# A delta-rule solve: diagonal blocks of 16 by substitution on VectorE, the last three doubling levels on TensorE

## The chip, the cores and the metric

The kernel runs on one core of a Trainium2 chip. The time is the device time of one launch in microseconds (us), the median of several runs. One execution of the kernel was also recorded by the hardware profiler; its rows are what this document reads. In them PE is TensorE, PEld its weight loads, DVE is VectorE, ACT ScalarE, POOL GpSimd and SP the engine that issues most transfers.

## The reference

One layer of a hybrid decoder on 512 tokens of width 1024: RMSNorm, one input projection, three kinds of heads side by side (softmax attention with forget gates, "fox"; retention; gated delta rule, "GDN"), an output projection, then a routed mixture of 32 experts. The part at issue is in the GDN heads, 4 heads, with the sequence cut into chunks of C = 64:

```
lower = where(strict, (kb @ k^T) * decay, 0)          # per head and chunk, 64 x 64
a_mat = lower + eye(64)
sol   = triangular_solve(a_mat, [v*beta | kb*exp(gc)], lower, unit_diagonal)
u0, w = split(sol)                                    # then a scan over the chunks
```

## The kernel before

**Granules.** The input projection is the first long stretch of TensorE work. It is cut into 30 granules (two for each of 15 groups of up to 260 columns; 8 more follow for the output projection). The product is taken in three terms from a high and a low part of activations and weights. Each granule is 48 matmuls of 256 columns (kind "n": tokens in rows, four tiles b = 0 to 3) or 24 of 512 (kind "t", turned: b = 0 and 1), line 792. Groups 12 (granules 24, 25) and below down to 8 are "n", groups 13 and 14 (26 to 29) "t". For each granule, SP loads the raw weights into a ring of three buffers, ScalarE copies the high part (`whi`, line 1255), GpSimd subtracts to get the low part (`wlo`, line 1555, "wlo(g)" for granule g). `wlo(g + 2)` is issued in GpSimd's turn g; TensorE waits for wlo(g) before granule g, and SP waits for `wlo_done` of granule g - 3 before it loads g.

**Tasks between granules.** `AFTER[g]` lists tasks behind granule g. All engines walk through the same list in the same order, each doing its part of every task, and meet through semaphores and through PSUM banks that are handed out in the order of the lists (`tensor_orders`). "evac" moves a group's result out of PSUM. Those of the solve, in which two token tiles of 128 (a pair, pr = 0 or 1, each tile holding two chunks for each of the four heads) are treated together:

- "dec", "decx" and GpSimd's `masked`: the decay matrices `Dm` and their strict form `Ym`.
- "prep": TensorE forms KK and QK; VectorE writes `Nm` (= lower, transposed), then starts the inverse with blocks of two, adds the identity and transposes (`uinit`), and writes `attnT`. GpSimd waits for `uinit` before its wlo, and afterwards multiplies `qT` by the row decays.
- "lv", level 0 to 5: with Y = N X and X' = X + U (mask Y), the size of the inverted blocks doubles from 2 to 64. 32 small matmul passes for Y, a mask on VectorE, 32 for X', a sum and two transposes on VectorE. One level stands between two granules.
- "fin": the inverse times the right sides (`wT`, `u0`).

Pair 0: "prep" behind granule 17, levels behind 18 to 23. Pair 1: "prep" behind 24, levels behind 25 to 29. On GpSimd, the rotation of the retention queries and keys (`rotary`, lines 1595 to 1600, six operations each) belongs to turns 21 (rq) and 23 (rk). In the turn whose list has "fin" of pair 0, it first does `masked` for tiles 2 and 3; in the turn with "prep" it waits for that task's signal before wlo.

VectorE links dependent operations with `link(...)`: the operation signals a semaphore, and the engine waits for it before the next.

After the projection come fox attention with the GDN scan and retention, the output projection, routing, and the experts in 16 pairs, whose weights (96 MB) are loaded as TensorE frees their buffers.

Of the kernel before, what the change touches and what calls it, by code (L numbers as in the profile page):

```python
# [23 lines left out]
F32 = mybir.dt.float32  # L24
# [27 lines left out]
LEVELS = 6  # L52
HB = P // 2
# [45 lines left out]
for _i in range(LEVELS):  # L99
    AFTER[18 + _i].append(("lv", 0, _i))  # L100
AFTER[23] += [("dec", 2), ("dec", 3), ("decx", 2)]
AFTER[24] += [("fin", 0), ("prep", 2)]
for _i in range(LEVELS - 1):
    AFTER[25 + _i].append(("lv", 1, _i))
AFTER[26].append(("silu",))
AFTER[29] += [("lv", 1, LEVELS - 1), ("fin", 1)]
# [18 lines left out]
def tensor_orders():  # L125

    a, b = [], []
    for g in range(GR_IN):
# [3 lines left out]
        for task in AFTER[g]:  # L132
# [80 lines left out]
def constant_table():  # L213
# [46 lines left out]
def build(nc, consts, x, turned, lead, w_in, foxb, alog, dtb, gnw, w_out, n2w, rgw, rgb, rew, reb,  # L260
# [13 lines left out]
    with ExitStack() as ctx:  # L274
# [17 lines left out]
        nM = const("nM", "p (l n) -> p l n", dict(l=LEVELS - 1))  # L292
# [64 lines left out]
        small = at("small", [P, 1024], R9 + 16 * KB)  # L357
        attnT = at("attnT", [P, T, NH, P], R5)
# [10 lines left out]
        UP, DN = slice(0, HB), slice(HB, P)  # L369
        rqT = at("rqT", [P, 2, S], R4)  # L370
# [19 lines left out]
        def sml(a, n):  # L390
            return small[:, a:a + n]
# [27 lines left out]
        vb_done = sem("vb_done"); s_bw = sem("s_bw"); s_cB = sem("s_cB"); s_gB = [sem(f"s_gB{t}") for t in range(T)]; xe_done = sem("xe_done")  # L419
# [106 lines left out]

        cbd = nc.dram_tensor("cbd", [2, NH * T, P], F32, kind="Internal")
# [49 lines left out]
        def _(sp):  # L577
# [177 lines left out]
        def _(pe):  # L755
# [85 lines left out]
            def task(k):  # L841
# [37 lines left out]
                elif k[0] == "lv":  # L879
                    _, pr, lv = k  # L880
                    for i in range(2):
                        t = 2 * pr + i
                        if lv:
# [11 lines left out]
                    for i in range(2):  # L895
# [4 lines left out]
                        elif lv:  # L900
                            pe.wait_ge(u_turned, 2 * (LEVELS - 2) * pr + 2 * (lv - 1) + i + 1)
# [1409 lines left out]
```

## Time and profile before

| what | value |
|---|---|
| median of 3 runs (lowest, highest) | 591.59 us (591.48, 592.23) |
| span of the profiled execution | 589.4 us |
| between span and median | 2.2 us |
| TensorE busy | 562.9 us, 96% of the span |
| VectorE, ScalarE, GpSimd busy | 259.9, 192.8, 183.1 us |
| moved by DMA | 152.67 MB |

The span runs from the first to the last recorded instruction; a program's time holds a little more. The profile has no time of its own for the execution beyond the span. Times of single instructions are counted from the span's start. A busy share says how long an engine had work, not whether it set the end.

### The profile page before, as it was taken

Reading aid. Unit: us, or ns where it says so; the run is one execution under the profiler, and the core shown is the slowest. Engines: PE = TensorE matmul, PEld = TensorE weight load, DVE = VectorE, ACT = ScalarE, POOL = GpSimd, SP = SyncE. Lnnn points to the kernel's source line nnn. Section 1 sums busy time; section 2 is a strip of 40 time slices with the busy share of each in tenths; the row PEclk is TensorE's granted clock in tenths of the full one; section 3 lists DMA queues with packets and bytes.
Section 4 is the critical chain, followed back from the end, with each engine's and each line's share of the span. In section 5 each row is a group of like instructions: output and inputs, shape, how many; then the busy total and the mean of one; then the engine's idle time right before and its main releaser. Section 6 shows DMA issues by size and latency. Waiting matters only on the chain.

```text
span 589.4 us, 11310 instructions
## 1 busy us (share of the span) xinstructions
PE 562.9 (96%) x4579; PEld 431.1 (73%) x4579; DVE 259.9 (44%) x622; ACT 192.8 (33%) x409; POOL 183.1 (31%) x126
## 2 busy tenths in 40 slices
PE   8999999999999999999999999989999999978894
PEld 7988887999999888666789997556566656644541
DVE  6698543782258333765421174223223323221126
ACT  6655455622124523356444312111111211110113
POOL 3443434273567534333552101111211111210021
PEclk9999999999999999999999999999999999999998
DMA  8866543422220310016989588999999999999986
GB/s 333 350 206 175 165 149 87 140 73 74 72 61 15 97 52 33 2 33 275 402 251 392 215 332 312 410 425 426 425 424 428 422 427 423 425 425 426 415 331 233
DMA packets 32083, 152.67 MB, mean 259 GB/s; under 512 B 8759, under 2 KB 12511, under 8 KB 25376
## 3 DMA queue, kind: packets, MB, share of 16 engines
q1 hardware_dynamic: 27360, 143.77, 63.2%
q0 software_dynamic: 4528, 8.15, 3.7%
q8 instruction: 37, 0.61, 0.4%
q14 instruction: 14, 0.11, 0.1%
q10 hardware_dynamic: 144, 0.03, 0.0%
HBM read 143.78 MB, written 16.27 MB: 272 GB/s over the span
## 4 chain that ended last, share of the span: by engine, by line
PE 76%; DMA 14%; DVE 4%; issue 2%; ACT 1%; POOL 1%; SPq 0%; DVEq 0%; POOLq 0%; ACTq 0%
PE bank L792 33%; PE bank L839 8%; DMA w<-in_expert_w_dram 8%; PE bank L1226 7%; DMA xg<-h2d,tok 6%; PE bank L1185 5%; PE bank L1200 5%; PE bank L817 2%; PE bank L1124 2%; PE bank L1138 2%; PE bank L1118 1%; PE bank L1238 1%; PE bank L1094 1%; PE bank L943 1%; PE bank L1010 1%
## 5 line engine op out<-in xcount | busy, mean ns | idle before, releaser
L1555 POOL TENSOR_TENSOR wlo<-raw,whi 128x1024 fp32r<-128x1024 f32 (+1 forms) x24 | 59.2, 2467 | 79.4 <-ACT whi L1255 75.3
L1682 POOL DMA_INDIRECT yd<-oy,dst x15 | 15.2, 1011 | 163.2 <-DVE oy L2217 152.5
L1200 PE MATMUL bank<-w,xT 128*64 128x256 f32 x512 | 58.1, 380 | 4.0 <-DMA w<-in_expert_w_dram 4.0
L1226 PE MATMUL bank<-w,hidT 128*64 128x512 f32 x256 | 58.5, 598 | 1.4 <-ACT hidT L1532 1.4
L1185 PE MATMUL bank<-w,xT 128*64 128x256 f32 x512 | 58.1, 380 | 1.7 <-issue 1.7
L792 PE MATMUL bank<-wlo,hHi 128*128 128x256 f32 (+2 forms) x192 | 55.9, 291 | 0.0
L1185 PEld LDWEIGHTS bank<-w,xT 128*64 128x64 f32 x512 | 36.9, 137 | 26.0 <-issue 10.1
L1200 PEld LDWEIGHTS bank<-w,xT 128*64 128x64 f32 x512 | 36.5, 137 | 22.9 <-DMA w<-in_expert_w_dram 4.9
L2195 DVE SCALAR_TENSOR_TENSOR hid<-bank,slot,sa 128x256 f32<-128x256 f32 x16 | 10.8, 673 | 93.1 <-issue 90.6
L792 PE MATMUL bank<-whi,hHi 128*128 128x256 f32 (+1 forms) x176 | 50.4, 287 | 0.0
L792 PE MATMUL bank<-whi,hLo 128*128 128x256 f32 (+1 forms) x176 | 49.6, 282 | 0.0
L792 PE MATMUL bank<-hHi,wlo 128*128 128x512 f32 x112 | 44.2, 394 | 0.0
L1527 ACT ACTIVATE sa<-bank,slot 128x256 f32<-128x256 f32 x16 | 7.6, 474 | 104.9 <-PE bank L1185 104.9
L1255 ACT ACTIVATE whi<-raw 128x1024 fp32r<-128x1024 f32 (+1 forms) x25 | 26.5, 1061 | 43.4 <-PE bank L792 40.0
L792 PE MATMUL bank<-hHi,whi 128*128 128x512 f32 x96 | 38.4, 400 | 0.5 <-POOL wlo L1555 0.5
L1226 PEld LDWEIGHTS bank<-w,hidT 128*64 128x64 f32 x256 | 16.9, 136 | 29.8 <-issue 27.4
L792 PE MATMUL bank<-hLo,whi 128*128 128x512 f32 x96 | 37.6, 391 | 0.0
L792 PE MATMUL bank<-whi_tight,hHi 128*128 128x256 f32 (+1 forms) x112 | 36.9, 329 | 0.5 <-issue 0.4
L792 PEld LDWEIGHTS bank<-wlo,hHi 128*128 128x128 f32 x192 | 36.2, 189 | 0.5
L792 PE MATMUL bank<-whi_tight,hLo 128*128 128x256 f32 (+1 forms) x112 | 35.1, 314 | 0.0
L1773 DVE SCALAR_TENSOR_TENSOR cacc<-bank,lead_in,cacc 128x511 f32<-128x511 f32 (+2 forms) x36 | 26.5, 747 | 18.2 <-ACT cacc L1337 17.1
L792 PEld LDWEIGHTS bank<-whi,hHi 128*128 128x128 f32 x176 | 33.2, 189 | 0.4
(385 smaller groups left out, 1146.3 us busy)
## 6 DMA issues: line engine op xcount, KB each, us to landing
w<-in_expert_w_dram SPq DMA_DIRECT2D x43, 2048.0 KB, 20.3
raw<-in_w_in_dram SPq DMA_DIRECT2D x24, 512.0 KB, 4.0
w<-in_expert_w_dram SPq DMA_DIRECT2D x10, 1024.0 KB, 7.8
yd<-zt SPq DMA_DIRECT2D x8, 512.0 KB, 5.1
yt<-yd SPq DMA_DIRECT2D x4, 1024.0 KB, 8.1
raw<-in_w_in_dram SPq DMA_DIRECT2D x6, 520.0 KB, 5.5
xt<-in_turned_dram SPq DMA_DIRECT2D x4, 512.0 KB, 6.8
X<-in_x_dram SPq DMA_DIRECT2D x4, 512.0 KB, 10.4
```

What stands on the lines that cost most here:

```text
L792: m = pe.matmul(o, l, r, start=(at == 0 and c == 0 and i == 0), stop=(at == parts - 1 and kc == chunks[-1] and i == 2), skip_group_check=True)
L817: m = pe.matmul(tiles[b][:, 0:w], l, r, start=(kc == 0 and i == 0), stop=(kc == KC - 1 and i == 2), skip_group_check=True)
L839: return pe.matmul(o, l, r, start=True, stop=True)
L1124: m = pe.matmul(pb[0][:, at + a:at + b], rows[:, t, :, :], TG[:, t, q:q + 1, a:b], start=(t == 0), stop=(t == T - 1), skip_group_check=True)
L1138: m = pe.transpose(pb[1 + c // 4][:, (c % 4) * P:(c % 4 + 1) * P], xg[s][:, c * P:(c + 1) * P], ident)
L1185: m = pe.matmul(pb[3][r, 0:FF], xT[:, c, r], w1[u % 4][:, e, c * FF:(c + 1) * FF], start=(c == 0), stop=(c == KC - 1), skip_group_check=True)
L1200: m = pe.matmul(pb[7][r, 0:FF], xT[:, c, r], w3[u % 4][:, e, c * FF:(c + 1) * FF], start=(c == 0), stop=(c == KC - 1), skip_group_check=True)
L1226: m = pe.matmul(pb[5 + n][r, :], hidT[:, c, r], w2[s][:, n, (2 * e + c) * 512:(2 * e + c + 1) * 512], start=(c == 0), stop=(c == 1), skip_ ...
L1255: e.activation(high_of(g), raw_of(g), ACT.Copy).then_inc(whi_done, 1)
L1555: pool.tensor_tensor(low_of(g), raw_of(g), high_of(g).bitcast(F32), ALU.subtract).then_inc(wlo_done, 1)
L1682: pool.indirect_dma_start(yd.ap()[:, :], bass.IndirectOffsetOnAxis(ap=dst_i[o][:, 0:1].bitcast(U32), axis=0), oy[o][:, :], None, bounds_ch ...
L1773: j = dve.scalar_tensor_tensor(out=a[:, s:S], in0=psum(name)[:, 0:S - s], scalar=PCW[:, 3 - s, blk:blk + 1], in1=a[:, s:S], op0=ALU.mult, ...
```

## The change

The inverse of each 16 x 16 diagonal block is now computed by VectorE, and the doubling starts from blocks of 16, so levels 0, 1 and 2 go for both pairs.

- "prep" masks the diagonal blocks out of `Nm` (`blk16`) and folds them with two reductions into `diag`, 128 partitions x 8 (two tiles, four heads) x 16. SP writes it to DRAM (`nbd`, 64 KB) and reads it back in eight transfers, each broadcasting one group of 16 rows to the 16 partitions that hold it, 8 KB to a partition (`spread`, over the place of `Ym` and `Dm`). So each partition holds all 16 rows of its own block.
- "solve" runs the substitution, step b = 1 to 15: a multiplication of 8 x b elements, whose second operand steps by 512 bytes through `spread`, and a reduction of 8 x (b + 1). Every operation is linked to the one before it. Two masked multiplications and two transposes then give `Uc` and `Xc` for level 3.
- `AMID` allows a task inside a granule, behind one of its tiles. Level 3 of pair 0 stands in the middle of granule 21, level 4 behind it, level 5 behind 22; "fin" and pair 1's "prep" move from behind 24 to behind 23; level 3 of pair 1 stands in the middle of granule 27, level 4 behind it, level 5 behind 28, "fin" behind 29.
- GpSimd's turn with "prep" waits for `rows_done` in place of `uinit`. SP's part (`blocks_round`) stands behind its loads of granules 21 and 27.

```diff
@@ -96,14 +98,25 @@
-for _i in range(LEVELS):
-    AFTER[18 + _i].append(("lv", 0, _i))
-AFTER[23] += [("dec", 2), ("dec", 3), ("decx", 2)]
-AFTER[24] += [("fin", 0), ("prep", 2)]
-for _i in range(LEVELS - 1):
-    AFTER[25 + _i].append(("lv", 1, _i))
+AFTER[18].append(("solve", 0))
+AMID = {g: {} for g in range(GR_IN)}
+AMID[21][1] = [("lv", 0, 3)]
+AFTER[21].append(("lv", 0, 4))
+AFTER[22] += [("lv", 0, 5), ("dec", 2), ("dec", 3), ("decx", 2)]
+AFTER[23] += [("fin", 0), ("prep", 2)]
+AFTER[24].append(("solve", 1))
...
-AFTER[29] += [("lv", 1, LEVELS - 1), ("fin", 1)]
+AMID[27][0] = [("lv", 1, 3)]
+AFTER[27].append(("lv", 1, 4))
+AFTER[28].append(("lv", 1, 5))
+AFTER[29].append(("fin", 1))
+BLOCKS_AT = {21: 0, 27: 1}
+def tasks_of(g):
+    return [k for b in sorted(AMID[g]) for k in AMID[g][b]] + AFTER[g]
...
@@ -228,10 +241,11 @@
-    put("nM1", -((row % 2 == 0) & (blk == row + 1)).astype(np.float32))
+    put("blk16", -(row // SB == blk // SB).astype(np.float32))
+    put("unit16", -(row % SB == np.arange(SB)[None, :]).astype(np.float32))
...
-    for n in range(LEVELS - 1):
+    for n in range(SOLVED, LEVELS - 1):
...
@@ -367,6 +385,8 @@
+        spread = at("spread", [P, SB, 2 * NH, SB], R4 + 12 * KB)
+        eights = lambda a: sml(a, 2 * NH * SB).rearrange("p (c n) -> p c n", c=2 * NH)
...
@@ -401,6 +419,7 @@
+        diag, inv, prods = eights(640), eights(768), eights(896)
...
@@ -524,6 +543,7 @@
+        nbd = nc.dram_tensor("nbd", [2, P, 2 * NH * SB], F32, kind="Internal")
...
@@ -622,15 +642,28 @@
                                  cbd.ap()[0:1].rearrange("o (t h) p -> o h t p", h=NH)[:, h].broadcast_to([P, T, P])
-                                 ).then_inc(s_cB, 16)
+                                 ).then_inc(s_spread, 16)
 
...
 
+            def blocks_round(pr):
+                sp.wait_ge(rows_done, pr + 2)
+                sp.dma_start(nbd.ap()[pr], small[:, 640:768]).then_inc(s_bw, 16)
+                for t in (2 * pr, 2 * pr + 1):
+                    wait_read(sp, ("QK", t))
+                sp.wait_ge(s_bw, 32 + 16 * (pr + 1))
+                for d in range(P // SB):
+                    src = nbd.ap()[pr:pr + 1, d * SB:(d + 1) * SB, :].rearrange("o k n -> o (k n)")
+                    sp.dma_start(spread[d * SB:(d + 1) * SB, :, :, :].rearrange("p k c n -> p (k c n)"),
+                                 src.broadcast_to([SB, SB * 2 * NH * SB])).then_inc(s_spread, 16)
             sp.wait_ge(zero_set, 1)
...
                 granule(g)
+                if g in BLOCKS_AT:
+                    blocks_round(BLOCKS_AT[g])
                 if g == 11:
...
@@ -880,7 +913,7 @@
-                        if lv:
+                        if lv > SOLVED:
...
@@ -897,8 +930,8 @@
-                        elif lv:
-                            pe.wait_ge(u_turned, 2 * (LEVELS - 2) * pr + 2 * (lv - 1) + i + 1)
+                        elif lv > SOLVED:
+                            pe.wait_ge(u_turned, 2 * (LEVELS - 2 - SOLVED) * pr + 2 * (lv - 1 - SOLVED) + i + 1)
...
@@ -922,7 +955,7 @@
-                    granule(g)
+                    granule(g, between=lambda b: [task(k) for k in AMID[g].get(b, ())])
...
@@ -1606,7 +1639,7 @@
                     if ("prep", t) in AFTER[g]:
-                        pool.wait_ge(uinit, t + 2)
+                        pool.wait_ge(rows_done, t // 2 + 2)
                 if ("decx", 0) not in AFTER[g]:
...
@@ -1882,14 +1915,12 @@
-                        dve.tensor_tensor(Yc[i][UP, :, :], Nm[i][UP, :, UP], half(const("nM1"), UP), ALU.mult)
-                        j = dve.tensor_tensor(Yc[i][DN, :, :], Nm[i][DN, :, DN], half(const("nM1"), DN), ALU.mult)
+                        for r in (UP, DN):
+                            j = dve.tensor_tensor(Xc[i][r, :, :], Nm[i][r, :, r], half(const("blk16"), r), ALU.mult)
...
-                        j = dve.tensor_tensor(Uc[i], Yc[i], id64.unsqueeze(1).broadcast_to([P, NH, HB]), ALU.add)
-                    link(j)
-                    for i in range(2):
-                        dve.transpose(Xc[i], Uc[i]).then_inc(uinit, 1)
+                        j = dve.tensor_reduce(diag[:, NH * i:NH * i + NH, :], Xc[i].rearrange("p h (d n) -> p h n d", n=SB), AX_X, ALU.add)
+                    j.then_inc(rows_done, 1)
...
@@ -1898,10 +1929,26 @@
+                elif k[0] == "solve":
+                    pr = k[1]
+                    unit = const("unit16").unsqueeze(1).broadcast_to([P, 2 * NH, SB])
+                    dve.tensor_copy(inv[:, :, 0:1], unit[:, :, 0:1])
+                    link(dve.tensor_copy(prods, unit))
+                    dve.wait_ge(s_spread, 16 * NH + 16 * (P // SB) * (pr + 1))
+                    for b in range(1, SB):
+                        link(dve.tensor_tensor(prods[:, :, 0:b], inv[:, :, 0:b], spread[:, 0:b, :, b].rearrange("p k c -> p c k"), ALU.mult))
+                        link(dve.tensor_reduce(inv[:, :, b], prods[:, :, 0:b + 1], AX_X, ALU.add))
+                    places = const("blk16", "p (d n) -> p d n", dict(n=SB)).unsqueeze(1).broadcast_to([P, NH, HB // SB, SB])
+                    for i in range(2):
+                        rows = inv[:, NH * i:NH * i + NH, :].unsqueeze(2).broadcast_to([P, NH, HB // SB, SB])
+                        j = dve.tensor_tensor(Uc[i].rearrange("p h (d n) -> p h d n", n=SB), rows, places, ALU.mult)
+                    link(j)
+                    for i in range(2):
+                        dve.transpose(Xc[i], Uc[i]).then_inc(uinit, 1)
...
-                        mask = nM[:, lv, :].unsqueeze(1).broadcast_to([P, NH, HB])
+                        mask = nM[:, lv - SOLVED, :].unsqueeze(1).broadcast_to([P, NH, HB])
...
```

The rest of the diff names the new constants, semaphores and views, makes `tasks_of` the list that the bank order and VectorE walk, and makes fox attention wait for the renamed semaphore of the cB loads.

## Rows read from the trace of the kernel before

**Rows 1.** The page: DMA rate in 40 slices, and the chain by engine.
```profile
GB/s 333 350 206 175 165 149 87 140 73 74 72 61 15 97 52 33 2 33 275 402 251 392 215 332 312 410 425 426 425 424 428 422 427 423 425 425 426 415 331 233
...
PE 76%; DMA 14%; DVE 4%; issue 2%; ACT 1%; POOL 1%; SPq 0%; DVEq 0%; POOLq 0%; ACTq 0%
```

**Rows 2.** TensorE's timeline: start, duration (us), instructions merged where alike.
```profile
2.00 5.87 PE L918 MATMUL bank<-zt 128*128 128x256 bf16 x30 [2.00 <-DVE zt L1720]
...
123.38 0.37 PE L792 MATMUL bank<-whi,hHi 128*128 128x256 f32 x1
...
129.25 0.33 PE L839 MATMUL bank<-Xm,Nm 64*64 64x64 f32 x4
...
137.40 1.15 PE L839 MATMUL bank<-Xm,Nm 64*64 64x64 f32 x32
...
139.69 0.38 PE L792 MATMUL bank<-whi,hHi 128*128 128x256 f32 x1
...
186.16 0.36 PE L792 MATMUL bank<-whi_tight,hHi 128*128 128x256 f32 x1
...
194.38 0.50 PE L792 MATMUL bank<-hHi,whi_tight 128*128 128x512 f32 x1
...
200.12 0.45 PE L839 MATMUL bank<-Xm,Nm 64*64 64x64 f32 x8
```

**Rows 3.** VectorE's timeline, behind the masks of "prep", pairs 0 and 1.
```profile
125.42 0.76 DVE L1889 TENSOR_TENSOR Xm<-Ym,CT 128x256 f32<-128x256 f32 x2
...
187.67 0.76 DVE L1889 TENSOR_TENSOR Xm<-Ym,CT 128x256 f32<-128x256 f32 x2
```

**Rows 4.** VectorE's timeline in the routing: linked operations; TG steps by 16 bytes.
```profile
342.83 0.29 DVE L2097 TENSOR_TENSOR rtB<-rtB,rtA 128x128 f32<-128x128 f32 x1
343.16 0.29 DVE L2098 TENSOR_TENSOR rtB<-rtB,CT 128x128 f32<-128x128 f32 x1
...
352.59 0.22 DVE L2146 TENSOR_TENSOR rtA<-rtA 128x64 f32<-128x64 f32 x1
...
353.16 0.28 DVE L2148 TENSOR_TENSOR rtA<-rtA,TG 128x64 f32<-128x64 f32 x1
```

**Rows 5.** The page: DMA issues, KB each, median us to landing.
```profile
cbd<-small SPq DMA_DIRECT2D x2, 8.0 KB, 3.3
```

**Rows 6.** Tile cB: issues (ns min/median/max, first and last start us), landings.
```profile
L623 SPq DMA_DIRECT2D cB<-cbd x4: 438/507/508, 102.2 to 103.8; - x4
...
DMA to landing us min/median/max: 4.7/5.3/6.1
```

**Rows 7.** VectorE's timeline, beside GpSimd's operations of rows 8.
```profile
45.97 2.41 DVE L1801 SCALAR_TENSOR_TENSOR small<-small 128x32 f32<-128x32 f32 x1
...
173.95 7.39 DVE L1869 TENSOR_SCALAR Dm<-mix,small 128x128 f32<-128x128 f32 x8
...
189.16 2.12 DVE L1897 SCALAR_TENSOR_TENSOR attnT<-bank,small,Dm 128x128 f32<-128x128 f32 x8
```

**Rows 8.** GpSimd's timeline.
```profile
45.92 2.41 POOL L1555 TENSOR_TENSOR wlo<-raw,whi 128x1024 fp32r<-128x1024 f32 x1 [2.05 <-ACT whi L1255]
...
139.20 2.38 POOL L1555 TENSOR_TENSOR wlo<-raw,whi 128x1024 fp32r<-128x1024 f32 x1 [4.91 <-ACT whi L1255]
...
174.33 1.11 POOL L1595 TENSOR_TENSOR rtmp<-rk,CT 128x512 f32<-128x512 f32 x1
...
180.00 1.26 POOL L1600 TENSOR_TENSOR rk<-rtmp,rtmp 128x512 f32<-128x512 f32 x1
...
189.31 2.41 POOL L1555 TENSOR_TENSOR wlo<-raw,whi_tight 128x1024 fp32r<-128x1024 f32 x1 [3.84 <-DVE Xm L1892]
191.67 2.51 POOL L1572 TENSOR_TENSOR qT<-qT,mix 128x512 f32<-128x512 f32 x2
...
201.42 2.39 POOL L1555 TENSOR_TENSOR wlo<-raw,whi_tight 128x1024 fp32r<-128x1024 f32 x1 [4.86 <-ACT whi_tight L1255]
```

**Rows 9.** Busy time by window: PE, PEld, DVE, ACT, POOL, PEclk, DMA share, GB/s.
```profile
581.50:586.00 4.50, 0.00 (x0) 0.00 (x0) 4.40 (x9) 2.46 (x6) 0.00 (x0) 0.76 0.43 162
```

More of the change, by code:

```diff
@@ L52 @@
 LEVELS = 6
+SB = 16
+SOLVED = 3
 HB = P // 2
@@ L131, in tensor_orders @@
             (b if g == 2 else a).extend(("y", g // 2, n) for n in range(T if kind == "n" else 2))
-        for task in AFTER[g]:
+        for task in tasks_of(g):
             if task[0] == "rb":
@@ L203 @@
 for _name, _n in [("ident", P), ("eps", 1), ("eps128", 1), ("ones", P), ("iota", 2 * CAP), ("tok1", T), ("thr", 8),
-                  ("desc", NE), ("gdesc", NG), ("rankm", P), ("tri", P), ("strict", P), ("negmask", P), ("nM1", HB), ("id64", HB),
-                  ("cos", T * 32), ("sin", T * 32), ("nM", (LEVELS - 1) * HB), ("dm", NH * S)]:
+                  ("desc", NE), ("gdesc", NG), ("rankm", P), ("tri", P), ("strict", P), ("negmask", P), ("blk16", HB), ("unit16", SB), ("id64", HB),
+                  ("cos", T * 32), ("sin", T * 32), ("nM", (LEVELS - 1 - SOLVED) * HB), ("dm", NH * S)]:
     CONST[_name] = (_at, _n)
@@ L291, in build @@
         ones, eps = const("ones"), const("eps")
-        nM = const("nM", "p (l n) -> p l n", dict(l=LEVELS - 1))
+        nM = const("nM", "p (l n) -> p l n", dict(l=LEVELS - 1 - SOLVED))
         id64 = const("id64")
@@ L357, in build, with sml @@
         small = at("small", [P, 1024], R9 + 16 * KB)
+        def sml(a, n):
+            return small[:, a:a + n]
         attnT = at("attnT", [P, T, NH, P], R5)
@@ L388, in build @@
         ssn, rn, ssx4 = keep[:, 88:104], keep[:, 104:120], keep[:, 120:136]
-        def sml(a, n):
-            return small[:, a:a + n]
         GAB = sml(0, 32).rearrange("p (t n) -> p t n", t=T)
@@ L418, in build @@
         cum_done = sem("cum_done"); rows_done = sem("rows_done"); cexp_done = sem("cexp_done")
-        vb_done = sem("vb_done"); s_bw = sem("s_bw"); s_cB = sem("s_cB"); s_gB = [sem(f"s_gB{t}") for t in range(T)]; xe_done = sem("xe_done")
+        vb_done = sem("vb_done"); s_bw = sem("s_bw"); s_spread = sem("s_spread"); s_gB = [sem(f"s_gB{t}") for t in range(T)]; xe_done = sem("xe_done")
         um_low = sem("um_low"); u_turned = sem("u_turned"); sq_done = sem("sq_done"); root_done = sem("root_done"); ss_read = sem("ss_read"); kt_done = sem("kt_done")
@@ L1931, in _ @@
             for g in range(GR_IN):
-                for k in AFTER[g]:
+                for k in tasks_of(g):
                     task(k)
@@ L1957, in _ @@
                         if u == 0:
-                            dve.wait_ge(s_cB, 16 * NH)
+                            dve.wait_ge(s_spread, 16 * NH + 32 * (P // SB))
                             dve.wait_ge(rot_done, 2)
```

## Prediction

> **What bounds the kernel now.** I read the forty slices and the chain of waits first [rows 1]. The chain lies on TensorE for 76% of the span. From about slice 25 the DMA engines move some 425 GB/s, so the expert stage is bound by weight transfers, but these are released by semaphores that TensorE's progress sets. Time won or lost between 120 and 235 us should therefore reach the end one for one. I read that stretch in the timelines of TensorE, VectorE and GpSimd [rows 2, 3, 7, 8]. TensorE does not idle there: a granule of the normal kind takes 5.87 us (123.38 to 129.25), one of the turned kind 5.74 (194.38 to 200.12), and between granules stands one doubling level, 137.40 to 139.69, so 2.29 us [rows 2]. VectorE and GpSimd have gaps of some us between tasks, and those gaps are what the change draws on.
>
> **What goes.** Levels 0, 1 and 2 of two pairs: 6 x 2.29 = 13.7 us of TensorE [rows 2]. Their VectorE work (masks, sums, transposes) hid in VectorE's gaps and gives nothing. The nM1 mask, the identity sum and the two transposes in "prep" are replaced by a blk16 mask of the same shape and two reductions, at the price of the two operations of 128x256, 0.76 us [rows 3]. The kept levels 3 to 5 cost what they did; putting level 3 inside a granule costs a break that the present ones have too.
>
> **The new chain behind "prep".** rows_done comes 0.76 us after the last mask: 125.42 + 0.76 = 126.2 for pair 0; for pair 1, 187.67 + 0.76 is 2.3 us after the granule behind "prep" started (186.16) [rows 2, 3]. I call that start T0. SP then writes 64 KB to DRAM: 3.3 us by the write of the cumulative rows [rows 5]. It reads back eight pieces, 1 MB in all. The cB loads move the same 1 MB, also broadcast from such a scratch, in four; the last is issued 1.6 us after the first and lands at most 6.1 us later [rows 6]: 7.7 us. The bounds are 4.7 (all eight overlap like the quickest quarter) and 10.1 (eight issues of 0.5 us, the last landing after 6.1). I take 7.7: the spread stands at 137.2 for pair 0, at T0 + 13.3 for pair 1. The raw loads queued behind these on SP have several us in hand, and so has wlo of the next granule, which now waits on rows_done instead of the transposes, so earlier.
>
> **The substitution.** Thirty operations, each waiting for the one before it. A linked operation of 128 elements recurs every 0.33 us at 0.29 of busy time, so a link adds 0.04; 64 elements are 0.22 busy [rows 4]. That gives 0.19 + 0.0011 per element. The multiplications have 8b elements, the reductions 8(b+1), for b = 1 to 15: 960 + 1080 = 2040. So 30 x 0.19 + 2040 x 0.0011 = 7.9 us. An operand with a step of 16 bytes costs 0.28 instead of 0.22 for 64 elements [rows 4]; the spread's step is 512 bytes, no row shows that one, and the same surcharge on 960 elements is 0.9. The bounds are 7.9 and, if the longer step is twice as dear, 9.7; I take 8.8, by the nearest row. Behind the loop come two 128x256 multiplications, 0.76, and the first transpose, for which I take half of that: 1.2 us until level 3 may begin [rows 3].
>
> **The shared port.** This is what decides. While GpSimd runs an operation of two SBUF operands, a VectorE operation that reads two SBUF tensors waits for its end: L1801, 32 elements wide, took 2.41 us from 45.97, beside the wlo operation from 45.92 to 48.33 [rows 7, 8]. Between back-to-back GpSimd operations VectorE gets one operation in: eight that need 0.27 us each took 7.39 beside the rotary [rows 7]. A PSUM operand is free of it: attnT, eight in 2.12 us, ran beside wlo from 189.31 [rows 7, 8]. The levels that go read PSUM; the multiplications inv x spread read SBUF twice. Each wlo that falls into the loop costs it 2.2 us.
>
> **Pair 0.** TensorE now reaches level 3 at 123.38 + 3.5 x 5.87 = 143.9. The wlo of granule 21 begins 1.8 us after granule 19 (139.20 against 137.40), so at 135.1 + 1.8 = 136.9, and ends at 139.3; that of granule 22 begins 1.3 after granule 20 (201.42 against 200.12), at 142.3 [rows 2, 8]. The loop starts at 139.3, takes 8.8 and loses 2.2: 150.3; with the tail 151.5. Stall 7.6 us. With the spread at its early bound (134.2) it does 2.7 us of steps before the first lock and ends at 148.6: 4.7. With the late one (139.9) 8.2.
>
> **Pair 1.** "prep" moves from behind granule 24 to behind 23, so rotary(rk), wlo(25) and qT change their order on GpSimd. There it is: wlo(25), which waits for rows_done, T0 + 2.3 to 4.7; rotary 6.9 (174.33 to 181.26) to 11.6; qT 2.5 to 14.1; wlo(26) 2.4 to 16.5, and 16.7 with the slots that VectorE takes; wlo(27) straight behind, to 19.2 [rows 8]. TensorE wants wlo(26) at T0 + 2 x 5.87 = 11.7 and waits 5.0 us. In the kernel before, rotary(rk) was over long before "prep". VectorE gets two multiplications in between these operations (0.8 us of its 8.8) and is free from 19.3; wlo(28) locks it once more, since granule 26 ends at 22.5: 19.3 + 8.0 + 2.2 + 1.2 = T0 + 30.7. Without any wait TensorE would be at level 3 of pair 1 at 11.7 + 5.74 + 2.87 = 20.3. So pair 1 costs 10.4 us, 5.0 of it before granule 26 and 5.4 at level 3. Early bound 9.3 (more slots used), late bound 10.8.
>
> **The clock.** Between 581.5 and 586, with TensorE idle, the granted clock reads 0.76 on the mean, so it fell from its full level (2.4 GHz) to the half within the stretch, after some 2.3 us of it [rows 9]. Nothing follows there, so the nearest row for what a fall costs is the start: thirty matmuls of 256 columns took 5.87 us, 0.20 each, where the 48 of a granule come at 0.12 [rows 2] (the column reads 1.00 even there, so this is read from the durations alone). That is 30 x 0.075 = 2.2 us lost. After 7.6 us of idling I expect level 3 to start at the lower level and take this 2.2. After the wait before granule 26 the same loss would only shorten the wait at level 3, which then leaves 3.2 us, and I count no second one. The bounds are 0 and 4.4.
>
> **The sum.** -13.7 + 7.6 + 10.4 + 2.2 = +6.5 us. The profiled span is 589.4, with the remaining 2.2 us up to the median of 591.59 lying around it; 589.4 + 6.5 + 2.2 = 598.1. All early bounds with no clock loss: -13.7 + 4.7 + 9.3 = +0.3, less 0.9 + 0.9 if the strided step costs nothing: -1.5. All late bounds: -13.7 + 8.2 + 10.8 + 4.4 + 1.8 = +11.5.
>
> **Rivals.** Faster: the lock does not hold a chain that gives the port up every 0.3 us, and GpSimd fits between its operations. Then pair 0 stands at 137.2 + 8.8 + 1.2 = 147.2, a stall of 3.3; pair 1 at T0 + 13.3 + 10.0 = 23.3, earlier than TensorE, which still waits 5.0 for wlo(26): -13.7 + 3.3 + 5.0 = -5.4, some 586.2 us, 588.4 with a clock loss. For it: short operations never met GpSimd in a long chain here. Against it: L1801 was short and lost 2.2 [rows 7]. The point where it decides is the sum of both pairs' waits passing 13.7.
>
> Slower yet: each of the eight reads fills only 16 partitions, so they could go through one after another at a fraction of the full rate. Taking a quarter of 425 GB/s [rows 1], 1.05 MB last 9.9 us, with 2 to start 11.9: the spread lands at 141.4 and T0 + 17.5. Pair 0 then stalls 141.4 + 8.8 + 2.2 + 1.2 - 143.9 = 9.7, pair 1 is free to start only at 19.2 and costs 19.2 + 8.8 + 2.2 + 1.2 - 20.3 = 11.1: -13.7 + 9.7 + 11.1 + 2.2 = +9.3, 600.9 us. No row here shows a large load into 16 partitions, for or against.
> The Trainium skill (SBUF — State Buffer, "Door 1: The DMA port swizzle") says that partitions 0 to 15 reach only four of the sixteen ports and measures 104 GB/s for them; by it this rival would be the forecast, an estimate of about 10 us of transfer, and no run here shows it yet.
>
> No change: DVE and GpSimd meet in kinder phases, for instance each solve loses one lock fewer (-2.2 each) and the clock holds (-2.2): -0.1 us. It needs three things together and gets little.
>
> **How the numbers follow.** The forecast 598.1 (own range 593.5 to 600) gets 0.48, the late spread 0.22 (600 to 604), the faster rival 0.22, no change 0.08. Around 0.2%, 1.2 us, is what a measurement can tell. Slower 0.70 plus a little of the last case's edge: 0.71; same 0.06; faster 0.23. The range runs from 587.5, which takes in most of the faster rival with a clock loss, to 603.
>
> **What would show it.** The spread's issue to landing times; L1801-like durations near 2.4 us among the multiplications of "solve"; idle time of TensorE before level 3 of both pairs, released by VectorE's transposes, and before granule 26, released by wlo; the granted clock after them. I am wrong if the multiplications keep 0.2 to 0.3 us beside GpSimd, or if wlo(26) is not late.

## The result, and the profile after

The changed kernel takes 599.33 us (median of four executions, 598.42 to 600.08), the kernel before 591.62 (four, 591.48 to 592.23). The ratio is 1.0126 with a 95% interval of 1.0107 to 1.0145: 7.7 us slower, where +6.5 was forecast. The profiled execution took 599.69 us, its span is 597.9 against 589.4. The forecast 598.1 and its own range of 593.5 to 600 held.

TensorE's waits between 110 and 300 us, by what ended them (us in total, times, longest):

```profile
PE bank L872 <- DVE Xm L1947: 10.1, 2, 7.1
PE bank L825 <- POOL wlo L1588: 5.2, 1, 5.2
PE bank L872 <- DVE vb L1992: 1.5, 1, 1.5
```

The first line is both pairs' level 3, waiting for the transpose behind the solve; the second is granule 26, waiting for its lower weights. The line of granules is L825 now (L792 before) and that of the levels L872 (L839).

TensorE's timeline, for [rows 2]: level 3 of pair 0 and its return, granule 26, level 3 of pair 1, and a place behind the stretch, the first of the retention products that waits for vb:

```profile
150.52 1.97 PE L872 MATMUL bank<-Xm,Nm 64*64 64x64 f32 x32 [7.13 <-DVE Xm L1947]
152.28 1.92 PE L872 MATMUL bank<-Ym,Xm 64*64 64x64 f32 x32
...
157.60 1.15 PE L872 MATMUL bank<-Xm,Nm 64*64 64x64 f32 x32
...
198.74 0.79 PE L825 MATMUL bank<-hHi,whi_tight 128*128 128x512 f32 x1 [5.19 <-POOL wlo L1588]
...
212.16 1.17 PE L872 MATMUL bank<-Xm,Nm 64*64 64x64 f32 x32 [2.97 <-DVE Xm L1947]
...
218.84 1.15 PE L872 MATMUL bank<-Xm,Nm 64*64 64x64 f32 x32
...
249.00 0.49 PE L872 MATMUL bank<-rqT,rkT 64*128 64x128 f32 x4 [1.47 <-DVE vb L1992]
```

TensorE is at level 3 of pair 0 at 150.52 - 7.13 = 143.39 (143.9 in the prediction), and at that of pair 1 when it has waited twice. T0, the start of granule 24, is 181.87.

VectorE's timeline, for [rows 3, 7]: the reductions of "prep", then the first, the held and the last multiplications of both substitutions, and what follows the first:

```profile
125.31 1.11 DVE L1922 TENSOR_REDUCE small<-Xm 128x64 f32<-128x256 f32 x2
...
138.53 0.48 DVE L1939 TENSOR_TENSOR small<-small,spread 128x8 f32<-128x8 f32 x1 [9.47 <-DMA spread<-nbd]
...
141.67 0.26 DVE L1939 TENSOR_TENSOR small<-small,spread 128x56 f32<-128x56 f32 x1
...
142.22 2.13 DVE L1939 TENSOR_TENSOR small<-small,spread 128x64 f32<-128x64 f32 x1
...
149.23 0.76 DVE L1944 TENSOR_TENSOR Xm<-small,CT 128x256 f32<-128x256 f32 x2
150.02 0.77 DVE L1947 STREAM_TRANSPOSE Xm<-Xm 128x256 f32<-128x256 f32 x2
...
196.48 2.24 DVE L1939 TENSOR_TENSOR small<-small,spread 128x8 f32<-128x8 f32 x1 [9.37 <-DMA spread<-nbd]
...
198.96 2.15 DVE L1939 TENSOR_TENSOR small<-small,spread 128x16 f32<-128x16 f32 x1
...
208.38 2.12 DVE L1939 TENSOR_TENSOR small<-small,spread 128x120 f32<-128x120 f32 x1
```

The spread's issues and landings, for [rows 6] (ns of an issue min/median/max, first and last start):

```profile
L659 SPq DMA_DIRECT2D spread<-nbd x16: 325/420/884, 128.6 to 190.7; - x16
...
DMA to landing us min/median/max: 2.9/4.9/6.7
```

GpSimd's timeline beside it, for [rows 8]:

```profile
141.81 2.42 POOL L1588 TENSOR_TENSOR wlo<-raw,whi 128x1040 fp32r<-128x1040 f32 x1 [2.83 <-ACT whi L1288]
...
184.56 2.39 POOL L1588 TENSOR_TENSOR wlo_tight<-raw,whi_tight 128x1024 fp32r<-128x1024 f32 x1 [7.78 <-DVE small L1922]
186.91 1.17 POOL L1628 TENSOR_TENSOR rtmp<-rk,CT 128x512 f32<-128x512 f32 x1
...
193.91 2.48 POOL L1605 TENSOR_TENSOR qT<-qT,mix 128x512 f32<-128x512 f32 x2
196.36 2.33 POOL L1588 TENSOR_TENSOR wlo<-raw,whi_tight 128x1024 fp32r<-128x1024 f32 x1
198.65 2.41 POOL L1588 TENSOR_TENSOR wlo_tight<-raw,whi_tight 128x1024 fp32r<-128x1024 f32 x1
...
207.70 2.57 POOL L1588 TENSOR_TENSOR wlo<-raw,whi_tight 128x1024 fp32r<-128x1024 f32 x1 [6.64 <-ACT whi_tight L1288]
```

Lay the two lists beside each other: each multiplication of over 2 us ends within 0.15 us of the end of a wlo (142.22 + 2.13 and 141.81 + 2.42; 196.48 + 2.24 and 196.36 + 2.33; 198.96 + 2.15 and 198.65 + 2.41), save the last, which ends at 210.50 against 210.27. A multiplication of 56 elements that met none took 0.26.

The granted clock in windows (us, TensorE busy with its instructions, clock, DMA share, GB/s), which never left 1.00 between 120 and 300 us before:

```profile
146.00:148.00 2.00, 0.00 (x0) 1.00 0.51 193
148.00:150.00 2.00, 0.00 (x0) 0.58 0.00 0
150.00:152.00 2.00, 1.48 (x28) 0.50 0.00 0
...
196.00:198.00 2.00, 0.00 (x0) 0.52 0.45 172
198.00:200.00 2.00, 1.26 (x3) 0.50 0.27 27
...
214.00:216.00 2.00, 2.00 (x28) 0.50 0.00 0
...
252.00:254.00 2.00, 2.00 (x11) 0.50 0.00 0
```

In this stretch it fell from 2.4 to 1.2 GHz four times: about 148 to 155, 196 to 203, 213 to 217 and 250 to 254. What each cost is the time between two marks, less the same stretch at the full level (a level 2.29, half a granule of 2.87 or a whole of 5.74): 157.60 - 150.52 - 5.16 = 1.9 us; from 198.74 to TensorE's arrival at level 3 (209.19), less 8.61 = 1.8; 218.84 - 212.16 - 5.16 = 1.5. The fourth follows a wait of only 1.5 us.

The ledger to the key transposes of the fox heads (240.96 after, 235.55 before, both measured from the start of granule 18, at 123.27 and 123.38) is +5.5 us: waits 7.1 + 5.2 + 3.0 = 15.3, clock 1.9 + 1.8 + 1.5 = 5.2, so by the remainder 15.0 us were taken away. Behind it come 2.3 us: a retention product waits 1.5 us where it waited 0.8, and the fourth fall takes 1.6 (249.00 to the same product of the next head group at 269.04 is 20.0 us, 242.94 to 261.34 before is 18.4). From there to the end the difference hardly grows, +7.7 to +8.5 in the spans.

### The profile page after: what moved, and what is told of

Its sections match the earlier page's. It is cut to its first block, busy times and chain, and to the rows that moved or that the text cites. A ratio compares the mean times of both kernels' runs of the same rounds, so it can differ in the third digit from the quotient of the medians.

```text
span 597.9 us, 10572 instructions
## 1 busy us (share of the span) xinstructions
PE 555.8 (93%) x4195; PEld 425.0 (71%) x4195; DVE 266.6 (45%) x654; ACT 192.8 (32%) x409; POOL 182.9 (31%) x126
## 4 chain that ended last, share of the span: by engine, by line
PE 61%; DMA 21%; DVE 11%; issue 3%; SPq 1%; POOL 1%; ACT 1%; POOLq 0%; DVEq 0%; ACTq 0%
PE bank L825 26%; DMA xg<-h2d,tok 8%; DMA w<-in_expert_w_dram 8%; PE bank L872 6%; PE bank L1259 5%; PE bank L1218 4%; PE bank L1233 4%; DVE small L1939 3%; DMA spread<-nbd 2%; PE bank L850 2%; PE bank L1157 2%; PE bank L1171 2%; DMA yd<-oy,dst 1%; PE bank L1151 1%; DVE small L1940 1%
## 5 line engine op out<-in xcount | busy, mean ns | idle before, releaser
L1218 PEld LDWEIGHTS bank<-w,xT 128*64 128x64 f32 x512 | 37.3, 137 | 27.7 <-issue 12.3
L825 PE MATMUL bank<-wlo,hHi 128*128 128x256 f32 (+2 forms) x192 | 56.0, 292 | 0.0
L825 PE MATMUL bank<-whi,hHi 128*128 128x256 f32 (+1 forms) x176 | 50.6, 288 | 0.0
L825 PE MATMUL bank<-whi,hLo 128*128 128x256 f32 (+1 forms) x176 | 49.8, 283 | 0.0
L825 PE MATMUL bank<-hHi,wlo 128*128 128x512 f32 x112 | 44.9, 401 | 0.0
L825 PE MATMUL bank<-hHi,whi 128*128 128x512 f32 x96 | 38.4, 400 | 0.5 <-POOL wlo L1588 0.5
L825 PE MATMUL bank<-hLo,whi 128*128 128x512 f32 x96 | 37.6, 391 | 0.0
L825 PE MATMUL bank<-whi_tight,hHi 128*128 128x256 f32 (+1 forms) x112 | 36.8, 329 | 0.5 <-issue 0.4
L825 PEld LDWEIGHTS bank<-wlo,hHi 128*128 128x128 f32 x192 | 36.5, 190 | 0.5
L825 PE MATMUL bank<-whi_tight,hLo 128*128 128x256 f32 (+1 forms) x112 | 35.1, 314 | 0.0
L825 PEld LDWEIGHTS bank<-whi,hHi 128*128 128x128 f32 x176 | 33.4, 190 | 0.3
```

Source lines behind the costliest of these rows:

```text
L825: m = pe.matmul(o, l, r, start=(at == 0 and c == 0 and i == 0), stop=(at == parts - 1 and kc == chunks[-1] and i == 2), skip_group_check=True)
L1218: m = pe.matmul(pb[3][r, 0:FF], xT[:, c, r], w1[u % 4][:, e, c * FF:(c + 1) * FF], start=(c == 0), stop=(c == KC - 1), skip_group_check=True)
```

## The experiments

The theory throughout: the loss is VectorE's solve (the substitution with its transfers), which starts when the spread lands and is held by GpSimd's operations on SBUF, plus the late wlo of granule 26, plus what the clock gives up after the waits. The rivals: the transfers are the cause; the clock alone is; or the waits are interchangeable, so that removing one shows the next. The kernel before took 591.92, 592.02 and 591.41 us beside the three sets of runs (e1 to e4, e5 to e8, e9 to e11). Waits and falls of the clock are counted below between 110 and 300 us. In the expert stage the profiles of e1 and e6 hold two more falls, those of e2, e3, e8 and e10 one, of 3.4 us each (447 to 568 us), and the others none, besides the one at the very end that all have; what they cost was not measured.

**e1: the rotation of the retention keys (`rotary(rk)`) moved on GpSimd from turn 23 to turn 27, behind wlo(29).**

```diff
-                elif k == ("evac", GIDX["za"]):
+                elif k == ("evac", GIDX["fq"]):
                     rotary(rk, 2)
```

> The changed kernel with GpSimd's rotation of the retention keys moved from its turn 23 to its turn 27, behind wlo(29). My theory: the wait before granule 26 (5.2 us) and its clock loss (1.9) go, but the wait at level 3 of pair 1 grows from 3.0 to about 7.8 us, because the solve itself, from 'prep' through the transfer and thirty linked operations, is then what is late; in all some 2 us are won, 597 us. Rival, that the order on GpSimd is a cost of its own beside the solve: the 7 us are won in full, 592 us.

Measured 596.75 us, ratio to the kernel before 1.0062 (1.0035 to 1.0088). TensorE's waits:

```profile
PE bank L872 <- DVE Xm L1947: 14.8, 2, 7.7
PE bank L872 <- DVE vb L1992: 1.5, 1, 1.5
```

The wait for wlo is gone, and 4.7 us of its 5.2 reappear at level 3 of pair 1, now 7.7 where it was 3.0; three falls of the clock are left. The order on GpSimd set the wait for wlo(26), and that wait stood in front of one for VectorE, as the prediction's 5.0 and 5.4 had it. So what was gained is what the solve of pair 1 gained, since TensorE waits for it either way: level 3 starts at T0 + 27.7 (209.67, T0 = 181.98) where it was T0 + 30.3. Without the rotation one multiplication of that loop is held where three were, though the loop begins 0.8 us later behind T0. VectorE's timeline, the one that is held:

```profile
200.53 2.42 DVE L1939 TENSOR_TENSOR small<-small,spread 128x56 f32<-128x56 f32 x1
```

**e2: the inverse under construction in PSUM,** so that each multiplication reads one SBUF operand only.

```diff
+                    inv = psum(("QK", 2 * pr + 1))[:, 0:2 * NH * SB].rearrange("p (c n) -> p c n", c=2 * NH)
+                    wait_read(dve, ("QK", 2 * pr + 1))
                     dve.tensor_copy(inv[:, :, 0:1], unit[:, :, 0:1])
```

> The changed kernel with the partial inverse in a PSUM bank that is free during the solve, so that the multiplications read one SBUF operand in place of two. Theory of the shared port: every multiplication takes 0.2 to 0.4 us, none 2.2; the wait at level 3 of pair 0 falls from 7.1 to about 5.3 us, the one of pair 1 from 3.0 to 0 with its clock loss; the wait before granule 26 stays. About 593 us. Rival, that the late transfer alone sets the waits and the long multiplications only mark it: no change, 599 us. If reading PSUM costs each operation 0.07 us more, 594 to 595.

Measured 591.97 us (ten executions), ratio 0.9993 (0.9981 to 1.0006): 7.4 us less than the changed kernel, from one operand. The spread's row of the loop, of the changed kernel and then of this one (instructions, ns min/median/max):

```profile
L1939 DVE TENSOR_TENSOR small<-small,spread x30: 188/302/2241, 138.5 to 208.4; 128x8 f32<-128x8 f32 x2, 128x16 f32<-128x16 f32 x2, 128x24 f32<-128x24 f32 x2, 128x32 f32<-128x32 f32 x2
```

```profile
L1941 DVE TENSOR_TENSOR small<-bank,spread x30: 173/265/364, 139.0 to 202.9; 128x8 f32<-128x8 f32 x2, 128x16 f32<-128x16 f32 x2, 128x24 f32<-128x24 f32 x2, 128x32 f32<-128x32 f32 x2
```

No multiplication takes over 0.364 us, with the same wlo operations beside them. TensorE waits 5.2 us before level 3 of pair 0 (7.1), not at all before that of pair 1 (3.0), and still 5.1 for wlo(26). So the hold needs both inputs in SBUF, as the prediction's shared port had it. Taking it away is worth less than the prediction's faster rival gave (598.1 against 588.4, 9.7 us), and two differences stand in the trace: the spread lands later than in that sum and leaves 5.2 us at pair 0 where the rival had 3.3, and the clock falls twice where it had one fall. And 1.6 of the 7.4 us lie behind the stretch: TensorE waits 1.5 us for vb as in the changed kernel, but this time the clock doesn't fall behind it.

**e3: no substitution.** The loop and the DRAM round trip are left out and the unit matrix stands for the inverse.

```diff
-                if g in BLOCKS_AT:
-                    blocks_round(BLOCKS_AT[g])
...
-                    dve.wait_ge(s_spread, 16 * NH + 16 * (P // SB) * (pr + 1))
-                    for b in range(1, SB):
-                        link(dve.tensor_tensor(prods[:, :, 0:b], inv[:, :, 0:b], spread[:, 0:b, :, b].rearrange("p k c -> p c k"), ALU.mult))
-                        link(dve.tensor_reduce(inv[:, :, b], prods[:, :, 0:b + 1], AX_X, ALU.add))
+                    link(dve.tensor_copy(inv, unit))
...
```

> The changed kernel without the thirty operations of each solve and without the transfers to and from DRAM: the 16 x 16 blocks are taken as if their inverse were the identity; all else, the order of tasks too, is as changed. Theory: both waits at level 3 go (7.1 + 3.0) with their clock losses (1.9 + 1.5), the wait before granule 26 stays at 5 us with its loss: 586 us, 5 to 6 below the kernel before. Rival, that the reordering around the solve costs more than 7 us by itself: 590 or more.

Measured 585.10 us, ratio 0.9888 (0.9868 to 0.9907). What is left in TensorE's waits is wlo(26), 5.5 us, and vb, 1.5, with one fall of the clock. So 14.2 us lie between the two kernels. 1.6 of them are the fall behind the wait for vb, which does not come here although the wait is there; the other 12.6 hang on the substitution itself. Some 7 more (5.5 and a fall of 1.9) hang on the order of GpSimd's work and stand without any substitution.

**e4: TensorE kept busy in its waits,** by idle products of 256 columns, 64 and 26 before the two levels 3 and 47 before granule 26.

```diff
+            def stay_busy(name, n):
+                b, uses = BANK[name]
+                pe.wait_ge(free[b], uses)
+                idb = ident.bitcast(BF16)
+                for _ in range(n):
+                    pe.matmul(pb[b][:, 0:256], idb[:, 0:P], idb[:, 0:256], start=True, stop=True)
```

> The changed kernel with idle matmuls of 256 columns on TensorE in place of the waits: 64 ahead of level 3 of pair 0, 47 ahead of granule 26, 26 ahead of level 3 of pair 1, a little less than fills each wait at full rate. Theory of the clock: no fall of the granted clock at these three places, the waits themselves end when they did, and 1.9 + 1.9 + 1.5 us come back, less what the second lets the third wait grow: 594 to 596 us. Rival, that the falls cost nothing beyond the waits: 599 us.

Measured 596.67 us, ratio 1.0074 (1.0051 to 1.0097). TensorE's timeline at level 3 of pair 0, at T0 and at level 3 of pair 1:

```profile
143.69 7.16 PE L879 MATMUL bank<-CT 128*128 128x256 bf16 x64
151.02 1.15 PE L872 MATMUL bank<-Xm,Nm 64*64 64x64 f32 x32 [0.18 <-DVE Xm L1958]
152.23 1.15 PE L872 MATMUL bank<-Ym,Xm 64*64 64x64 f32 x32
...
180.61 0.37 PE L825 MATMUL bank<-whi,hHi 128*128 128x256 f32 x1
...
210.97 1.15 PE L872 MATMUL bank<-Xm,Nm 64*64 64x64 f32 x32 [2.07 <-DVE Xm L1958]
```

The level's first half takes 1.15 us again (1.97 after the idle wait). The falls at 148 and 196 us are gone, those at 212 and 250 stay. 2.7 us came back by the medians. Where they came back is in the marks. From granule 18 to T0 it is 1.7 us (56.89 against 58.60): the first fall alone, with level 3 of pair 0 starting no earlier. From T0 to level 3 of pair 1 it is nothing (30.36 against 30.29): the second fall is gone too, but the level waits for VectorE all the same. From there to the key transposes of the fox heads it is nothing again. So a fall is a cost of its own only where no other wait stands behind it; the first is shown to be one, and the second cost nothing here. The rest of the 2.7 lies behind the stretch (0.8 us of it in the two profiles) and was not followed.

**e5 and e6: the round trip.** e5 cuts the spread into eight pieces along the row, each to all 128 partitions (every partition then holds the rows of the first block, so the inverse is another one); e6 keeps the pieces of 16 partitions but reads them from different addresses of a weight, so that its numbers are not the block's.

```diff
-                    src = nbd.ap()[pr:pr + 1, d * SB:(d + 1) * SB, :].rearrange("o k n -> o (k n)")
-                    sp.dma_start(spread[d * SB:(d + 1) * SB, :, :, :].rearrange("p k c n -> p (k c n)"),
-                                 src.broadcast_to([SB, SB * 2 * NH * SB])).then_inc(s_spread, 16)
+                    src = nbd.ap()[pr:pr + 1, 2 * d:2 * d + 2, :].rearrange("o k n -> o (k n)")
+                    sp.dma_start(spread[:, 2 * d:2 * d + 2, :, :].rearrange("p k c n -> p (k c n)"),
+                                 src.broadcast_to([P, 2 * 2 * NH * SB])).then_inc(s_spread, 16)
```

In e6 the source of each piece alone changes, to `w_in[d * SB:(d + 1) * SB, 0:SB * 2 * NH * SB]`.

> The changed kernel with the same eight transfers and bytes, but each goes to all 128 partitions, 1 KB to a partition, in place of 16 partitions and 8 KB (every partition gets the rows of the first block, so the inverse is another one). If the few partitions of each transfer are what holds it to some 130 GB/s, the spread is complete about 6 to 7.5 us after the first issue, in place of 9.4 to 10. If the repeated reading of one small place in DRAM holds it, 9 to 10 us as now. The time hardly moves either way by the theory of the shared port (1 to 2 us), since the first steps run into wlo.

> The changed kernel with the eight transfers to 16 partitions, 8 KB each, as they are, but reading 128 different rows of a weight matrix in place of one scratch row sixteen times (the spread then holds weights, so the inverse is another one). If the few partitions hold the transfer, it stays at 9 to 10 us from the first issue; if the repeated reading of one place does, it falls to 6 or 7.

One execution each: 597.24 and 597.70 us, beside 592.02. The windows of pair 0's transfer (TensorE busy, clock, DMA share, GB/s) in the changed kernel, e5 and e6:

```profile
131.00:133.00 2.00, 2.00 (x19) 1.00 1.02 127
133.00:135.00 2.00, 2.00 (x19) 1.00 0.99 123
```

```profile
131.00:133.00 2.00, 2.00 (x19) 1.00 0.85 236
133.00:135.00 2.00, 2.00 (x19) 1.00 0.71 204
```

```profile
131.00:133.00 2.00, 2.00 (x19) 1.00 1.10 156
133.00:135.00 2.00, 2.00 (x19) 1.00 1.07 152
```

Into 16 partitions the queues are fully busy at a third of the 425 GB/s of [rows 1], whether the source is one block or many; into all partitions they move up to 236 GB/s and are not full. Yet from first issue to first multiplication it takes 8.6 and 8.9 us in e5, 9.3 and 9.0 in e6, 10.0 and 9.4 in the changed kernel, and the 6 to 7.5 us expected of e5 were missed by 1 to 3 us. Eight issues take 3.6 us, and seven of e5's pieces land 2.7 to 3.2 us behind their issues, so they are there 6.0 us after the first. The eighth lands 5.3 us behind its own (132.22 to 137.54), with the next raw load issued right behind it; whether that load holds it up was not tested. TensorE's waits are the same in all three, 10.0 or 10.1, 5.2 and 1.5. The loop of e5's pair 0 begins at 137.64, in the middle of the wlo of granule 21, and its first multiplication is held until 139.47; so an earlier start only meets another wlo. What the two lie below the changed kernel, 2.1 and 1.6 us, is about the fall behind the wait for vb, which comes in neither. The transfer rate is not the cause of the loss.

**e7: levels 3 and 4 one and a half granules later and level 5 one,** where by the theory the solve is done.

```diff
-AMID[21][1] = [("lv", 0, 3)]
-AFTER[21].append(("lv", 0, 4))
-AFTER[22] += [("lv", 0, 5), ("dec", 2), ("dec", 3), ("decx", 2)]
-AFTER[23] += [("fin", 0), ("prep", 2)]
+AFTER[22] += [("lv", 0, 3), ("dec", 2)]
+AMID[23][1] = [("lv", 0, 4), ("dec", 3)]
+AFTER[23] += [("lv", 0, 5), ("decx", 2), ("fin", 0), ("prep", 2)]
...
-AMID[27][0] = [("lv", 1, 3)]
-AFTER[27].append(("lv", 1, 4))
-AFTER[28].append(("lv", 1, 5))
-AFTER[29].append(("fin", 1))
+AFTER[28].append(("lv", 1, 3))
+AMID[29][0] = [("lv", 1, 4)]
+AFTER[29] += [("lv", 1, 5), ("fin", 1)]
```

> The changed kernel with the kept levels later: pair 0 levels 3, 4, 5 behind granule 22, inside 23, behind 23; pair 1 behind 28, inside 29, behind 29. By the theory the two waits at level 3 vanish (the solves are ready 27 to 30 us after 'prep', the places are now 29 us behind it), the wait before granule 26 stays with its clock loss: 599.3 - 7.1 - 1.9 - 3.0 - 1.5 = 585.8 us. Rival, that levels close together at the end of a stretch bring waits of their own: 588 to 592.

Measured 587.70 us, ratio 0.9925 (0.9908 to 0.9943). The waits for Xm fall from 10.1 to 1.9 us, the one for wlo stays at 5.2, one fall of the clock is left. The same work on VectorE, held as before, costs little where TensorE has granules to do meanwhile. The time is 1.9 us above what was expected. The wait that is left has its reason in the timelines: TensorE no longer stands still, so the next wlo comes before pair 0's solve is through (148.33) and holds it once more (2.19 us for 120 elements), and the rotation behind it holds the product of the tail (2.16 where 0.76 is its own time). Level 4 then waits 0.8 for Ym; on the other side the wait for vb is down to 0.8 with no fall behind it.

**e8: e7 and e1 together.**

> As the run before, and with the rotation of the keys on GpSimd moved to its turn 27. Theory: now the solve is not late, so the wait before granule 26 (5.2) and its clock loss (1.9) come back in full: 579 us, 12 to 13 below the kernel before. If the order on GpSimd was only a symptom, no gain on the run before.

Measured 583.77 us, ratio 0.9854 (0.9835 to 0.9874), 4.8 above what was expected. VectorE's timeline behind pair 1's loop:

```profile
202.63 0.29 DVE L1938 TENSOR_REDUCE small<-small 128x8 f32<-128x128 f32 x1
202.95 3.63 DVE L1942 TENSOR_TENSOR Xm<-small,CT 128x256 f32<-128x256 f32 x2
206.62 0.77 DVE L1945 STREAM_TRANSPOSE Xm<-Xm 128x256 f32<-128x256 f32 x2
```

The two products behind the loop took 3.63 us where they take 0.76: wlo (202.67 to 205.06) and the rotation that was moved there held them. TensorE waited 2.5 us for Xm there and 1.9 at pair 0 as in e7, and the clock fell once, behind the longer of the two.

**e9, e10, e11: e8 with the inverse in PSUM (as e2), with the rotation of the keys one granule later still (the edit below, against e8), and with both.**

```diff
-                elif k == ("evac", GIDX["fq"]):
+                elif k == ("lv", 1, 3):
                     rotary(rk, 2)
```

> The third levels 3 to 5 of e7 (a stretch later), the second rotary product behind granule 27 as in e8, and the inverse under construction in PSUM as in e2. Theory (what e8 kept, 4.4 us of waits for Xm and one fall of the clock of some 1.6, is VectorE's solve held by GpSimd; with the inverse in PSUM its 30 multiplications are not held, so it ends some 4 us earlier for each pair): both waits for Xm fall under 0.5 us and the fall at 208 to 212 us goes; 583.8 - 1.9 - 2.5 - 1.6 = 577.8, range 577 to 580. Rival (the tail's products read and write SBUF still, the late rotary holds them, and TensorE arrives before them all the same): the wait before the last pair's level 3 stays at 1.5 to 2.5 us with its fall, 580.5 to 582.

> As e8, with the second rotary product one turn later still, behind granule 28's lower weights, so that it can't lie beside the tail of the last pair's solve; the inverse is in SBUF. Theory: the tail (3.6 us in e8) is then held by the lower weights of granule 29 alone, about 2.1 us, in place of these and the rotary product; level 3 of the last pair waits 1.5 to 2.2 us in place of 2.5, and the fall of the clock stays: 583.8 - 0.6 = 583.2, range 582.5 to 584. Rival (the rotary product in the tail's way is what e8 lost all its 4 us by): the wait goes and the fall with it, 579.5 to 580.5.

> e9 with the second rotary product behind granule 28 as in e10. Theory: in e9 nothing waits for VectorE's solve any longer, so this gives the same as e9 within 0.5 us (577 to 580). Rival of e9 (the tail is still held by the rotary product): this one is 2 to 4 us faster than e9, and without a wait for Xm.

Measured 581.06 (ratio 0.9817, 0.9801 to 0.9834), 581.72 (0.9834, 0.9818 to 0.9851) and 580.70 us (0.9809, 0.9783 to 0.9836). TensorE's waits in e10, and then in e11:

```profile
PE bank L870 <- DVE Xm L1945: 3.5, 2, 1.9
...
PE bank L870 <- DVE vb L1990: 0.8, 1, 0.8
PE bank L870 <- DVE Ym L1954: 0.8, 1, 0.8
```

```profile
PE bank L870 <- DVE Ym L1956: 1.9, 1, 1.9
...
PE bank L870 <- DVE vb L1992: 0.8, 1, 0.8
```

With the inverse in PSUM no wait for Xm is left, as expected, yet e9 came out 1 us above its range: the solve ends earlier, level 3 of pair 0 as well, and so the scalings of "dec" behind it now lie beside the end of the rotation of the queries and a wlo (GpSimd busy from 150.50 to 159.72). Four of them took 4.55 us from 155.45, level 4 waited 1.85 us for its Ym behind them, and the clock fell there. e10 was expected at 582.5 to 584 and came out 0.8 below: it kept 3.5 us of waits for Xm (1.9 and 1.6), near what was expected, but the clock did not fall behind the second, and that fall had been counted. e11 is not to be told from e9, so in e9 the rotation of the keys was no longer in the way. The three lie 9.7 to 10.7 us below the kernel before and 17.6 to 18.6 below the changed one.

## Why the prediction was right, point by point

**The gain.** 13.7 us of levels was counted, and the ledger leaves 15.0. Of the 1.3 between them the timelines show 1.1. In the kernel before, levels 4 and 5 of pair 1 and "fin" stood back to back behind the last granule and took 9.65 us (224.06 to 233.71); apart they take 2.29, 3.09 and 3.57, 0.7 less. And 3.5 granules with no level between them take 20.12 us (123.27 to 143.39), where 3.5 x 5.87 is 20.55, 0.4 more. The last 0.2 was not settled.

**The start of the loop.** Three terms were off and partly cancel. The reductions of "prep" took 1.11 us for the pair, not 0.76 [rows 3]. From the write's issue to the first read's it took 2.1 us for pair 0 (126.45 to 128.55) and 2.5 for pair 1 (184.51 to 187.04), not 3.3. The write itself landed after 1.8 and 1.5; `blocks_round` also waits until attnT is written (128.48 and 186.55), a wait that the prediction did not have. The spread was in use 10.0 and 9.4 us behind its first issue, not 7.7: near the value of the late bound (10.1), short of the 11.9 of the rival. So the cB loads [rows 6], four to all 128 partitions, were a poor row for it; by e5 the few partitions account for 1.4 of the 2.3 us missing at pair 0 and 0.5 of the 1.7 at pair 1. The rest remains in e5, with eight issues and its late eighth piece. The sum had the loop begin at 139.3, after the wlo of granule 21, and it began at 138.53, inside it.
The Trainium skill (SBUF — State Buffer, "Door 1: The DMA port swizzle"), which was cited beside the rival with 104 GB/s for partitions 0 to 15, agrees with the trace in direction: 123 to 143 GB/s at full share here, for eight pieces that each fill another 16 partitions. It was the size of this term that was wrong, not the mechanism. That it hardly counted is because the loop would have waited for the wlo anyway (e5 shows the same waits).

**The substitution.** Predicted 8.8 us without holds. Pair 0's ran from 138.53 to 149.20, which is 10.7; less a hold of 1.9 (2.13 where pair 1's multiplication of the same 64 elements takes 0.27) and one of 0.3 at the first (0.48, in the end of the wlo from 136.60 to 138.98), 8.5. Pair 1's is 14.4 less 5.8, so 8.6. The price of the 512-byte step, by the nearest row, holds too: 64 elements take 0.27 against 0.22 for the reduction of the same size.

**The port.** 2.2 us a hold was predicted, 1.75 to 2.1 measured, one in pair 0, besides the 0.3, and three in pair 1 (5.8 us of its 14.4). The rival in which a chain of short operations is not held is refuted by these rows and by e2.

**The waits.** Pair 0: 7.6 predicted, 7.1 measured. Granule 26: 5.0 and 5.2; wlo(26) ended at 198.69 = T0 + 16.8, the moment in the sum (16.7). Level 3 of pair 1: 5.4 predicted, or 3.2 if the clock fell behind the wait before, and 3.0 measured, because TensorE, at the lower clock through granule 26, came to it later; the end of the solve was right, level 3 starts at 212.16 = T0 + 30.3 (30.7 predicted).

**The clock.** One loss of 2.2 us was counted; there were four, 1.9 + 1.8 + 1.5 + 1.6. The second did only shorten the wait at level 3, as the prediction said it would, and e4 shows it (T0 + 30.4 with no such fall). The third and the fourth were not foreseen (3.1 us), nor the 0.7 at vb. With them the sum comes out right partly by luck, since the levels, the waits of both pairs with the second fall, and the first fall came 2.5 us below it: +15.3 of waits and +6.8 of clock, less 15.0, and 0.7 for vb is +7.8, against -13.7 + 18.0 + 2.2 = +6.5.

**Past the stretch.** That nothing would be added after 235 us was wrong by 2.3 us. GpSimd's product of the mix with PGN starts at 239.98 behind the last wlo and, with what follows it, ends as VectorE scales Pf (a second scaling took 0.89 us, 0.29 before), and so vb is later. The order is read from the timelines; no experiment moved only that product. It is not the substitution: without it (e3) the wait is 1.5 us as well. e7 to e11, in which the wait is 0.8 again and no fall follows it, fit this but changed more than one thing.

## What to carry to other kernels

A serial chain of short VectorE operations that take both inputs from SBUF is as long as its own time plus most of each GpSimd operation on SBUF inputs that begins meanwhile (1.75 to 2.1 us of a wlo's 2.4). An accumulator in PSUM removes that at no cost in the chain: 8.5 us for pair 0's loop without holds, and 8.5 in e2; the kernel gained 7.4. When work leaves the bounding engine for a slower one, move its consumer as well: the same solve cost 10.1 us of waits where its result was wanted at once and 1.9 one and a half granules later (e7, 11.6 us gained in all). And price each wait of TensorE with the clock that it may lose behind it, 1.5 to 1.9 us here, unless another wait stands behind that takes the loss in (the second fall).

## What the runs showed that was not expected

The clock fell behind waits of quite different length. After 7.1 and 5.2 us it fell while TensorE was still waiting. But it also fell behind waits of 3.0 and 1.5 us in the changed kernel, 2.5 in e8 and 1.9 in e9 and e11, and in those TensorE was already going again (from 212.16, falling at 213.2; from 249.00, at 250.7; in e9 from 160.38, at 161.0). Waits of 1.6 and 1.9 us in e10, of 1.9 in e7 and of 2.5 in the expert stage of the kernel before (up to 530.73) drew no fall at all. The plainest case is the wait for vb, 1.5 us in all of these kernels: a fall follows it in the changed kernel, e1 and e4, none in e2, e3, e5 and e6. So the length of the wait alone does not decide; what does was not settled. It also means that 1.6 us can come or go between two variants whose edits leave that wait as it was. Each fall in the stretch lasted 3 to 7 us.

A DMA into 16 partitions of SBUF kept all queues busy at 123 to 156 GB/s, where pieces to 128 partitions moved 204 to 240 at a share of 0.7 to 0.85. Even so the megabyte was in use only 0.5 to 1.4 us earlier: seven pieces of eight had landed 6.0 us after the first issue, the eighth 2.5 us or more behind them.
